# Prompt attention: the coefficients of the probabilities for two heads at a time, the first pair ahead

## Chip, cores and metric

The kernel runs on one core of a Trainium2 chip. The core has five engines that work side by side and wait for one another by semaphores: TensorE (PE: products of matrices, transposes; its loads of weights are shown as PEld), VectorE (DVE), ScalarE (ACT), GpSimd (POOL) and SyncE (SP, which issues DMAs). The metric is the device time of one execution in microseconds, as the median of several runs.

## What is computed

One step of a hybrid layer for a prompt of 1024 tokens and a decode batch of 8 sequences with 4 tokens each: a recurrent mixer, an attention with three branches, and a convolutional feed-forward. The change touches only the attention of the prompt, 8 query heads of width 64 in 2 groups that share keys and values:

```
def masked_softmax(s, mask):
    s = jnp.where(mask, s.astype(jnp.float32), -jnp.inf)
    m = jnp.max(s, axis=-1, keepdims=True)
    e = jnp.where(mask, jnp.exp(s - m), 0.0)
    d = jnp.sum(e, axis=-1, keepdims=True)
    return e / jnp.where(d > 0, d, 1.0)
...
    g = jax.nn.sigmoid(gate_raw.astype(jnp.float32)).reshape(B, T, 3, NSA_KV_HEADS, NSA_GROUP)[..., None]
    o = g[:, :, 0] * o_cmp + g[:, :, 1] * o_slc + g[:, :, 2] * o_win
```

The three branches attend to compressed keys, to selected blocks of keys (with 1024 tokens and 16 blocks of 64, all of them are selected) and to a window of 512 keys. Each branch's probabilities are divided by their sum d and weighted by a gate g; gate over sum is the coefficient that this document speaks of, one number for each query and head.

## The kernel before

`prompt_attention` works in units. For each of the 2 groups there is one unit for the compressed branch (C), and then for each tile of 128 queries, 0 to 7, one for the selected branch (S0, S1, ...) and one for the window (W0, W1, ...): 17 units in a group, 32 dense ones (S and W) in all. A dense unit has 4 heads (R) and a width u.w of 128 for each block of keys: 128 to 1024 for S, at most 640 for W.

A unit goes through these steps:
- Scores on PE (`scores`, L802 to L807), in fills of the two score tiles in PSUM, `ps`: one fill of four heads up to a width of 256, two fills of two heads up to 512, four fills of one head above. So S0 to W1 have one fill, S2 to W3 two, S4 to W7 four.
- Maximum on DVE (`maximum`, L717), negated into `nm`.
- Exponential on ACT (`probabilities`, L630), from the score tile into `Pr[u.dense % 3]` in SBUF, with the sum of each head put into `den` by the same operation.
- Coefficients on DVE (`coefficients`, L730 and L731): for four heads at once, the reciprocal of `den` in place, a wait on that (`cd`), and the product with the gates into `cf`. The wait in front is for all four heads' exponentials.
- Scaling on GpSimd (`scale`, L587): one operation for each head, in place in `Pr`, in the order of the units.
- For each block of 128 keys ("back"): four transposes on PE, one for each head, into a tile `pt` of PSUM (`turn`, L826; with the first block, the transpose of head h waits for the scaling of head h), a copy of the high part on ACT (`high_of`, L644, or L640 for compressed probabilities), the remainder on DVE (`rest_of`, L739), and two products with the values on PE (`values`, L846 and L847), two backs later. W units of an even tile have one back more, for the compressed probabilities of two tiles.
- After the last back of a W unit: the two halves of the sum are copied out of PSUM by ACT (L651) and DVE (L744) and added by DVE (L751) (`both_halves`).

The order of all this is written out by hand. Stage i (one pass of the outermost loop) interleaves the backs of unit i with the "fronts" (fills: scores, maximum, exponential) of unit i+2, by `merged(i)`; PE, ACT and DVE all go through the same list. Behind the first entry of stage i, which is a front if there is one, DVE makes the coefficients of unit i+1. ACT is one fill behind: it does an exponential behind the next back's copy, or in front of the next front.

For example, the list of stage S5, where the fronts are those of S6, is: f0 b0 b1 f1 b2 f2 b3 b4 f3 b5.

Of the kernel before, what the change touches and what calls it, by code (L numbers as in the profile page):

```python
# [9 lines left out]
ALU = mybir.AluOpType  # L10
# [14 lines left out]
R = NH // NG  # L25
# [427 lines left out]
def prompt_attention(nc, io, keep, scratch, consts_sb):  # L453
# [6 lines left out]
    CMP, SLC, WND = 0, 1, 2  # L460
    AHEAD = 2
# [4 lines left out]
    units = []  # L466
    n_fills = n_heads = n_groups = n_dense = 0
    for g in range(NG):
        for kind, qt in [(CMP, 0)] + [(kind, qt) for qt in range(NQ) for kind in (SLC, WND)]:
            u = Unit()  # L470
# [39 lines left out]
    with ExitStack() as ctx:  # L510
# [7 lines left out]
        mask, cmask, eye, gates = keep["mask"], keep["cmask"], keep["eye"], keep["gates"]  # L518
# [5 lines left out]
        den = sb("den", [P, NU, R])  # L524
        cf = sb("cf", [P, NU, R])
        nmc, denc, cfc = (sb(n, [P, NG, R, NQ]) for n in ("nmc", "denc", "cfc"))
        half = sb("half", [64, 512])
# [9 lines left out]
        s_ready, max_ready, e_ready, c_ready, p_ready = (sem(n) for n in ("s_ready", "max_ready", "e_ready", "c_ready", "p_ready"))  # L537
# [44 lines left out]
        @block.gpsimd  # L582
        def _(pool):
            def scale(u):
                pool.wait_ge(c_ready, u.dense + 1)
                for h in range(R):
                    nc.gpsimd.tensor_scalar(Pr[u.dense % 3][:, h, 0:u.w], Pr[u.dense % 3][:, h, 0:u.w], cf[:, u.n, h:h + 1], None,  # L587
                                            ALU.mult).then_inc(p_ready, 1)

            def scale_compressed(u):  # L590
                pool.wait_ge(cc_ready, u.g + 1)
                p3 = Pc[u.g][:].rearrange("p r t n -> p (r t) n")
                nc.gpsimd.tensor_tensor(p3, p3, cfc[:, u.g].rearrange("p r t -> p (r t)").unsqueeze(2).to_broadcast([P, R * NQ, CB]),
                                        ALU.mult).then_inc(cp_ready, 1)

            for u in units:
                if u.kind == CMP:
                    scale_compressed(u)
                else:
                    scale(u)  # L600
# [75 lines left out]
        @block.vector  # L676
        def _(dve):
            for e in range(4):
                dve.wait_ge(kH_ready, e + 1)
                at = (slice(None), e // 2, slice(512 * (e % 2), 512 * (e % 2) + 512))  # L680
                nc.vector.scalar_tensor_tensor(KT[1][:, 1][at], pt[e % 3][:].rearrange("p b c -> p (b c)"), SCALE, KT[1][:, 0][at].bitcast(F32),
                                               ALU.mult, ALU.subtract).then_inc(kL_ready, 1)

            def second_low(i):
                if i == 1:
                    for a in range(2):
                        dve.wait_ge(vH_ready, a + 1)
                        nc.vector.tensor_tensor(V2[1][:, a, :, DK:P], vv[:, a, :, DK:2 * DK], V2[1][:, a, :, 0:DK].bitcast(F32), ALU.subtract
                                                ).then_inc(vL_ready, 1)
                elif i in (2, 3):  # L690
                    for h in range(2 * i - 4, 2 * i - 2):
                        dve.wait_ge(qH_ready, h + 1)
                        nc.vector.tensor_tensor(Q[1][64:128, h, :], qs[h % 2][64:128, :], Q[1][64:128, h, :].bitcast(F32), ALU.subtract
                                                ).then_inc(qL_ready, 1)

            cs, cd = Steps(dve, cs_step), Steps(dve, cd_step)

            def maximum(u, b):
                s = ps[(u.fill0 + b) % 2]
                dve.wait_ge(s_ready, u.fill0 + b + 1)  # L700
                if u.kind == CMP:
                    s3 = s[:].rearrange("p (x n) -> p x n", n=CB)
                    m = nmc[:, u.g, 2 * b:2 * b + 2].rearrange("p r t -> p (r t)")
                    cs(nc.vector.tensor_reduce(m, s3, AX.X, ALU.max))
                    cs(nc.vector.tensor_scalar(m, m, -BIG / 1e10, None, ALU.max))
                    nc.vector.tensor_tensor(Pc[u.g][:, 2 * b:2 * b + 2].rearrange("p r t n -> p (r t) n"), s3,
                                            m.unsqueeze(2).to_broadcast([P, 2 * NQ, CB]), ALU.subtract).then_inc(cs_ready, 1)
                    return
                if u.per == 4:
                    src = s[:].rearrange("p (b x) -> p b x", b=2)[:, :, 0:2 * u.w].rearrange("p b (i w) -> p b i w", i=2)  # L710
                    dst = nm[:, u.n, :].rearrange("p (b i) -> p b i", b=2)
                elif u.per == 2:
                    src = s[:].rearrange("p (b x) -> p b x", b=2)[:, :, 0:u.w]
                    dst = nm[:, u.n, 2 * b:2 * b + 2]
                else:
                    src, dst = s[:, 0:u.w], nm[:, u.n, b:b + 1]
                nc.vector.tensor_reduce(dst, src, AX.X, ALU.max, negate=True).then_inc(max_ready, 1)  # L717

            def coefficients(u):
                if u.kind == CMP:  # L720
                    dve.wait_ge(ce_ready, u.fills * (u.g + 1))
                    d = denc[:, u.g].rearrange("p r t -> p (r t)")
                    cd(nc.vector.tensor_reduce(d, Pc[u.g][:].rearrange("p r t n -> p (r t) n"), AX.X, ALU.add))
                    cd(nc.vector.tensor_scalar(d, d, 1e-30, None, ALU.max))
                    cd(nc.vector.reciprocal(d, d))
                    nc.vector.tensor_tensor(cfc[:, u.g], denc[:, u.g], gates[:, :, R * u.g:R * u.g + R].rearrange("p t r -> p r t"),
                                            ALU.mult).then_inc(cc_ready, 1)
                    return
                dve.wait_ge(e_ready, u.head0 + R)
                cd(nc.vector.reciprocal(den[:, u.n, :], den[:, u.n, :]))  # L730
                nc.vector.tensor_tensor(cf[:, u.n, :], den[:, u.n, :], gates[:, u.qt, 8 * u.kind + R * u.g:8 * u.kind + R * u.g + R],  # L731
                                        ALU.mult).then_inc(c_ready, 1)

            def rest_of(u, k):
                G = u.group0 + k
                dve.wait_ge(h_ready, G + 1)
                src = pt[G % 3][:].rearrange("p b c -> p (b c)")
                hi, lo = (PcH[:], PcL[:]) if u.pair and k == u.groups - 1 else (PTH[:, G % 3, :], PTL[:, G % 3, :])
                nc.vector.tensor_tensor(lo, src, hi.bitcast(F32), ALU.subtract).then_inc(l_ready, 1)  # L739

            def both_halves(u):
                a = u.g * NQ + u.qt
                dve.wait_ge(pv_ready, pv_before[u.n])
                nc.vector.tensor_copy(lower[:], acc[0:64, :]).then_inc(lower_ready, 1)  # L744
                dve.wait_ge(half_ready, a + 1)
                dve.wait_ge(lower_ready, a + 1)
                if a >= 2:
                    dve.wait_ge(oT_out[a % 2], 16 * (a // 2))
                for odd in range(2):
                    at = lambda x: x.rearrange("p (k o c) -> p k o c", k=2, o=2)[:, :, odd]  # L750
                    nc.vector.tensor_tensor(oT[a % 2][64 * odd:64 * odd + 64], at(lower[:]), at(half[:]), ALU.add).then_inc(oT_ready, 1)  # L751

            for i in range(-AHEAD, NU + 1):
                order = merged(i)
                turned = 0
                for n in range(max(1, len(order))):
                    if order:
                        what, k = order[n]
                        if what == "back":
                            rest_of(units[i], k)  # L760
                            turned += 1
                            if turned == 2 and units[i - 1].kind == WND:
                                both_halves(units[i - 1])
                        else:
                            maximum(units[i + AHEAD], k)
                    if n == 0:
                        if 0 <= i + 1 < NU:
                            coefficients(units[i + 1])
                if turned < 2 and 1 <= i <= NU and units[i - 1].kind == WND:
                    both_halves(units[i - 1])  # L770
                second_low(i)
# [2157 lines left out]
```

## Time and profile before

| | |
|---|---|
| median of 3 runs | 2477.19 us (2475.43 to 2477.25) |
| profiled execution | 2471.7 us, its span 2469.9 us |
| PE busy in the span | 2281.8 us (92%) |
| DVE busy | 1305.3 us (53%) |
| ACT busy | 946.9 us (38%) |
| GpSimd busy | 513.2 us (21%) |
| prompt attention, dense units | 1212 us to 1518 us of the span |

The profile is of one execution. Times in its rows are counted from the start of the span. A row of the timeline gives the start, the time taken, the engine, the line of the kernel, the operation with its output and input, and in square brackets the idle time of the engine before it with the instruction that ended it; a row with no bracket had next to none. Names are those of the program without buffer numbers: `a_Pr` are the probabilities, `a_PTH` and `a_PTL` the high part and the remainder of a transposed block, `a_nm` the maxima, `a_den` the sums, `a_cf` the coefficients.

### The profile page before, as it was taken

The page shows a single profiled execution, that of the slowest core. Times are in us where ns is not written, and L with a number is a line of the kernel's source. Part 1 is how long each engine was busy: PE and PEld are TensorE (multiplying, and loading weights), DVE is VectorE, ACT ScalarE, POOL GpSimd, SP SyncE. Part 2 cuts the span into 40 slices and gives each one's busy share as a digit, 9 for nine tenths or more (in the row PEclk, how much of TensorE's full clock was granted, in tenths as well). Part 3 has the DMA queues.
Part 4 walks back from the last instruction along what each step waited for, and adds up shares of the span by engine and source line. Part 5 has one row for each costly group of instructions (what it writes and reads, how often), then busy time and mean ns, then how long its engine had stood idle before and what let it go on. Part 6 is the DMA issues. An engine that isn't in the chain of part 4 may idle for free. (4 is left out here: it accounts for less than half of the span.)

```text
span 2469.9 us, 40234 instructions
## 1 busy us (share of the span) xinstructions
PE 2281.8 (92%) x15950; PEld 2044.5 (83%) x15950; DVE 1305.3 (53%) x2960; ACT 946.9 (38%) x1911; POOL 513.2 (21%) x877
## 2 busy tenths in 40 slices
PE   6999989999999999669788885989999999999999
PEld 6999987777877777558667674869999999989998
DVE  5123028867767767643576775453333343355555
ACT  4124124545545545412365664112222222144444
POOL 0000005333433333200277673100000000011110
PEclk9999999999999999879699997999999999999999
DMA  4125626745546453297110002321111111122223
GB/s 133 52 64 174 241 97 222 229 157 177 174 154 207 154 177 94 56 300 216 41 41 7 10 7 94 109 73 48 51 42 51 43 45 49 51 77 82 79 70 116
DMA packets 213285, 263.10 MB, mean 107 GB/s; under 512 B 32386, under 2 KB 180098, under 8 KB 203746
## 3 DMA queue, kind: packets, MB, share of 16 engines
q1 hardware_dynamic: 194376, 157.61, 21.2%
q0 software_dynamic: 18752, 103.37, 12.1%
q8 instruction: 103, 1.69, 0.3%
q14 instruction: 54, 0.44, 0.1%
HBM read 202.76 MB, written 65.05 MB: 108 GB/s over the span
## 5 line engine op out<-in xcount | busy, mean ns | idle before, releaser
L1453 PE MATMUL f<-hH,wH 128*128 128x352 f32 x1056 | 341.4, 323 | 5.2 <-DVE wL L1339 5.2
L1453 PE MATMUL f<-hL,wH 128*128 128x352 f32 x1056 | 339.1, 321 | 0.0
L1453 PE MATMUL f<-hH,wL 128*128 128x352 f32 x1056 | 338.8, 321 | 0.0
L2406 ACT CAST a_XTH<-cpt 64x256 fp32r<-64x256 f32 (+1 forms) x576 | 201.1, 349 | 148.5 <-PE cpt L2613 137.9
L2523 DVE TENSOR_TENSOR a_XTL<-cpt,a_XTH 64x256 fp32r<-64x256 f32 (+1 forms) x576 | 230.3, 400 | 32.4 <-ACT a_XTH L2406 24.1
L1468 PE MATMUL f<-wdH,aH 128*128 128x256 f32 (+1 forms) x792 | 225.1, 284 | 5.3 <-DVE aL L1391 4.6
L1468 PE MATMUL f<-wdH,aL 128*128 128x256 f32 (+1 forms) x792 | 224.3, 283 | 0.0
L1468 PE MATMUL f<-wdL,aH 128*128 128x256 f32 (+1 forms) x792 | 224.3, 283 | 0.0
L587 POOL TENSOR_SCALAR a_Pr<-a_Pr,a_cf 128x640 f32<-128x640 f32 (+7 forms) x128 | 204.2, 1613 | 72.5 <-DVE a_cf L731 72.4
L2628 PE MATMUL cph<-a_XTH,a_w1H 128*128 128x512 f32 x512 | 217.4, 425 | 0.0
L2628 PE MATMUL cph<-a_XTH,a_w1L 128*128 128x512 f32 x512 | 205.3, 401 | 0.0
L2628 PE MATMUL cph<-a_XTL,a_w1H 128*128 128x512 f32 x512 | 204.4, 399 | 0.0
L1453 PEld LDWEIGHTS f<-hH,wH 128*128 128x128 f32 x1056 | 198.8, 188 | 5.3 <-DVE wL L1339 5.3
L1453 PEld LDWEIGHTS f<-hL,wH 128*128 128x128 f32 x1056 | 198.9, 188 | 0.0
L1453 PEld LDWEIGHTS f<-hH,wL 128*128 128x128 f32 x1056 | 198.5, 188 | 0.0
L1391 DVE TENSOR_TENSOR aL<-a_aT,aH 128x1408 fp32r<-128x1408 f32 (+1 forms) x72 | 108.2, 1503 | 122.7 <-ACT aH L1280 122.7
L1339 DVE TENSOR_TENSOR wL<-raw,wH 128x1024 fp32r<-128x1024 f32 x44 | 53.8, 1225 | 225.2 <-ACT wH L1242 222.8
L2231 POOL DMA_INDIRECT a_X<-in_cache_nsa_kv,idx x64 | 62.9, 983 | 425.7 <-issue 351.3
L1468 PEld LDWEIGHTS f<-wdH,aH 128*128 128x128 f32 (+1 forms) x792 | 144.0, 182 | 6.8 <-DVE aL L1391 5.2
L1280 ACT CAST aH<-a_aT 128x1408 fp32r<-128x1408 f32 (+1 forms) x72 | 91.4, 1270 | 147.5 <-PE f L1468 147.4
L1468 PEld LDWEIGHTS f<-wdL,aH 128*128 128x128 f32 (+1 forms) x792 | 144.0, 182 | 0.7
L1468 PEld LDWEIGHTS f<-wdH,aL 128*128 128x128 f32 (+1 forms) x792 | 143.9, 182 | 0.7
(459 smaller groups left out, 5377.3 us busy)
## 6 DMA issues: line engine op xcount, KB each, us to landing
v_s<-a_X SPq DMA_DIRECT2D x32, 512.0 KB, 6.4
raw<-in_w_in POOLq DMA_DIRECT2D x12, 1024.0 KB, 5.9
a_V<-v_s SPq DMA_DIRECT2D x6, 2048.0 KB, 15.0
raw<-in_w_gate SPq DMA_DIRECT2D x22, 512.0 KB, 3.8
raw<-in_w_val SPq DMA_DIRECT2D x22, 512.0 KB, 3.8
wraw<-in_w_down SPq DMA_DIRECT2D x44, 256.0 KB, 3.8
z_tok<-stage SPq DMA_DIRECT2D x48, 128.0 KB, 3.5
a_akq<-hq SPq DMA_DIRECT2D x32, 192.0 KB, 5.5
```

What stands on the lines that cost most here:

```text
L587: nc.gpsimd.tensor_scalar(Pr[u.dense % 3][:, h, 0:u.w], Pr[u.dense % 3][:, h, 0:u.w], cf[:, u.n, h:h + 1], None, ALU.mult).then_inc(p_read ...
L1280: nc.scalar.copy(aH[:, h, :, 0:r], aT[:, NFH * h:NFH * h + NFH, t * P:t * P + r]).then_inc(aH_ready, 1)
L1339: nc.vector.tensor_tensor(wL[:, a], raw[:, a], wH[:, a].bitcast(F32), ALU.subtract).then_inc(wL_ready, 1)
L1391: nc.vector.tensor_tensor(aL[:, h, :, 0:r], aT[:, NFH * h:NFH * h + NFH, t * P:t * P + r], aH[:, h, :, 0:r].bitcast(F32), ALU.subtract).th ...
L1453: last = nc.tensor.matmul(bank[3 * a + n][:, 0:w], wp[:, a, k, :], hp[:, k, c0:c0 + w], start=(k + part == 0), stop=(k == KD - 1 and part ...
L1468: last = nc.tensor.matmul(bank[t % 3][0:r, 0:QW], ap[:, h, j, 0:r], wp[:, f, :], start=(f + part == 0), stop=(f == NF - 1 and part == 2))
L2231: nc.gpsimd.indirect_dma_start(X[j % 3][:, half].rearrange("p t n -> p (t n)"), None, cache, bass.IndirectOffsetOnAxis(ap=idx[:, 2 * u + h ...
L2406: nc.scalar.copy(turned(XTH, u, s, k, g, a), split(bank(at, k)[:], u, k, g, a)).then_inc(h_ready, 1)
L2523: last = nc.vector.tensor_tensor(turned(XTL, u, s, k, g, a), split(bank(at, k)[:], u, k, g, a), hi.bitcast(F32), ALU.subtract)
L2628: last = nc.tensor.matmul(out[:, :, 0:n], w[:, k, q, s, m * P:(m + 1) * P], x[:, s % 2, k, :, q:q + n], **flags)
```

## The change

The coefficients of a dense unit are made for heads 0 and 1, and for heads 2 and 3, each pair with its own wait for its two exponentials and its own increment of `c_ready`. GpSimd waits for the first before head 0 and for the second before head 2. For units of more than one fill, the first pair moves from the stage after the unit's scores into the stage of its scores: it stands behind the entry that follows the unit's third front for four fills (`n + 1`), and behind the second entry after its second front, or at the end of the stage if that comes first, for two fills (`n + 2`). The second pair stays where the coefficients were. In units of one fill both pairs stand there.

```diff
@@ scale, on GpSimd
-                pool.wait_ge(c_ready, u.dense + 1)
                 for h in range(R):
+                    pool.wait_ge(c_ready, 2 * u.dense + 1 + h // 2)
                     nc.gpsimd.tensor_scalar(Pr[u.dense % 3][:, h, 0:u.w], Pr[u.dense % 3][:, h, 0:u.w], cf[:, u.n, h:h + 1], None,
                                             ALU.mult).then_inc(p_ready, 1)
@@ coefficients, on DVE
-                dve.wait_ge(e_ready, u.head0 + R)
-                cd(nc.vector.reciprocal(den[:, u.n, :], den[:, u.n, :]))
-                nc.vector.tensor_tensor(cf[:, u.n, :], den[:, u.n, :], gates[:, u.qt, 8 * u.kind + R * u.g:8 * u.kind + R * u.g + R],
-                                        ALU.mult).then_inc(c_ready, 1)
+                for half in range(2):
+                    if (u.n, half) not in weighted:
+                        pair_coefficients(u, half)
+
+            weighted = set()
+
+            def pair_coefficients(u, half):
+                hs = slice(2 * half, 2 * half + 2)
+                at = 8 * u.kind + R * u.g + 2 * half
+                weighted.add((u.n, half))
+                dve.wait_ge(e_ready, u.head0 + 2 * half + 2)
+                cd(nc.vector.reciprocal(den[:, u.n, hs], den[:, u.n, hs]))
+                nc.vector.tensor_tensor(cf[:, u.n, hs], den[:, u.n, hs], gates[:, u.qt, at:at + 2], ALU.mult).then_inc(c_ready, 1)
@@ the list of a stage, on DVE
-                turned = 0
+                turned, early = 0, None
...
-                            maximum(units[i + AHEAD], k)
+                            u = units[i + AHEAD]
+                            maximum(u, k)
+                            if u.kind != CMP and u.fills > 1 and k == u.fills // 2:
+                                early = (n + 1 if u.fills == 4 else n + 2, u)
+                        if early is not None and n >= early[0]:
+                            pair_coefficients(early[1], 0)
+                            early = None
                     if n == 0:
                         if 0 <= i + 1 < NU:
                             coefficients(units[i + 1])
+                if early is not None:
+                    pair_coefficients(early[1], 0)
```

## Rows read from the trace of the kernel before

**Rows 1.** Start:end, length, busy of PE, PEld, DVE, ACT, POOL, PE's clock, DMA

```profile
1212.00:1518.00 306.00, 252.88 (x1438) 206.77 (x1437) 225.99 (x355) 183.16 (x412) 211.39 (x130) 0.93 0.06 18
```

**Rows 2.** Waits, same stretch: total us, times, longest

```profile
POOL a_Pr L587 <- DVE a_cf L731: 72.4, 24, 8.0
...
DVE a_PTL L739 <- ACT a_PTH L644: 52.5, 65, 5.0
...
PE pt L826 <- POOL a_Pr L587: 34.4, 36, 3.3
```

**Rows 3.** GpSimd's groups by shape: busy us, mean ns, idle before

```profile
L587 POOL TENSOR_SCALAR a_Pr<-a_Pr,a_cf 128x896 f32<-128x896 f32 x8 | 20.1, 2527 | 10.1 <-DVE a_cf L731 10.1
```

**Rows 4.** Groups of DVE's instructions, same stretch and columns

```profile
L717 DVE TENSOR_REDUCE a_nm<-s 128x1 f32<-128x640 f32 (+7 forms) x87 | 83.2, 956 | 5.6 <-PE s L807 4.5
...
L731 DVE TENSOR_TENSOR a_cf<-a_den,gates 128x4 f32<-128x4 f32 x32 | 9.0, 281 | 1.1
...
L730 DVE RECIPROCAL a_den<-a_den 128x4 f32<-128x4 f32 x32 | 5.4, 169 | 0.1
```

**Rows 5.** Timeline around S6: start us, us, instruction, idle before

```profile
1304.77 0.69 DVE L739 TENSOR_TENSOR a_PTL<-pt,a_PTH 128x512 fp32r<-128x512 f32 x1
...
1309.30 0.17 DVE L730 RECIPROCAL a_den<-a_den 128x4 f32<-128x4 f32 x1
...
1309.50 0.16 DVE L731 TENSOR_TENSOR a_cf<-a_den,gates 128x4 f32<-128x4 f32 x1
...
1309.76 17.49 POOL L587 TENSOR_SCALAR a_Pr<-a_Pr,a_cf 128x896 f32<-128x896 f32 x8 [5.07 <-DVE a_cf L731]
...
1317.35 0.33 PE L826 MATMUL pt<-ident,a_Pr 128*128 128x128 f32 x1 [0.67 <-POOL a_Pr L587]
...
1319.85 0.33 PE L826 MATMUL pt<-ident,a_Pr 128*128 128x128 f32 x1 [2.17 <-POOL a_Pr L587]
...
1320.83 0.69 DVE L739 TENSOR_TENSOR a_PTL<-pt,a_PTH 128x512 fp32r<-128x512 f32 x1 [2.54 <-ACT a_PTH L644]
```

**Rows 6.** Timeline of DVE, GpSimd and PE around S7 of the second group

```profile
1483.02 0.68 DVE L739 TENSOR_TENSOR a_PTL<-pt,a_PTH 128x512 fp32r<-128x512 f32 x1
...
1488.42 11.32 POOL L587 TENSOR_SCALAR a_Pr<-a_Pr,a_cf 128x1024 f32<-128x1024 f32 x4 [7.90 <-DVE a_cf L731]
...
1499.79 0.47 PE L826 MATMUL pt<-ident,a_Pr 128*128 128x128 f32 x1 [2.49 <-POOL a_Pr L587]
...
1500.92 0.69 DVE L739 TENSOR_TENSOR a_PTL<-pt,a_PTH 128x512 fp32r<-128x512 f32 x1 [5.03 <-ACT a_PTH L644]
```

**Rows 7.** Timeline of DVE: first remainders of S4, S5; one amid W3's stage

```profile
1277.58 0.69 DVE L739 TENSOR_TENSOR a_PTL<-pt,a_PTH 128x512 fp32r<-128x512 f32 x1 [1.36 <-ACT a_PTH L644]
...
1297.71 0.69 DVE L739 TENSOR_TENSOR a_PTL<-pt,a_PTH 128x512 fp32r<-128x512 f32 x1 [0.59 <-ACT a_PTH L644]
...
1272.52 0.69 DVE L739 TENSOR_TENSOR a_PTL<-pt,a_PTH 128x512 fp32r<-128x512 f32 x1 [0.26 <-ACT a_PTH L644]
```

**Rows 8.** Timeline of DVE: first remainders of S2, first and second group

```profile
1245.51 0.69 DVE L739 TENSOR_TENSOR a_PTL<-pt,a_PTH 128x512 fp32r<-128x512 f32 x1 [2.31 <-ACT a_PTH L644]
...
1399.04 0.69 DVE L739 TENSOR_TENSOR a_PTL<-pt,a_PTH 128x512 fp32r<-128x512 f32 x1 [1.69 <-ACT a_PTH L644]
```

**Rows 9.** Timeline of DVE: first remainders of S3 and S7, first group

```profile
1260.56 0.69 DVE L739 TENSOR_TENSOR a_PTL<-pt,a_PTH 128x512 fp32r<-128x512 f32 x1
...
1348.19 0.68 DVE L739 TENSOR_TENSOR a_PTL<-pt,a_PTH 128x512 fp32r<-128x512 f32 x1
```

**Rows 10.** Timeline of GpSimd and DVE: scalings, and output sums beside them

```profile
1299.08 5.61 POOL L587 TENSOR_SCALAR a_Pr<-a_Pr,a_cf 128x640 f32<-128x640 f32 x3
...
1301.00 1.00 DVE L751 TENSOR_TENSOR a_oT<-a_lower,a_half 64x256 f32<-64x256 f32 x1
...
1348.37 7.47 POOL L587 TENSOR_SCALAR a_Pr<-a_Pr,a_cf 128x640 f32<-128x640 f32 x4 [1.82 <-DVE a_cf L731]
...
1350.96 0.87 DVE L751 TENSOR_TENSOR a_oT<-a_lower,a_half 64x256 f32<-64x256 f32 x2
```

## Prediction

> **Names.** S6 is the unit of the selected branch for query tile 6, W6 the window unit that follows it; the order is S0, W0, S1, W1 and so on, once for each group of heads. While unit i is turned and used, the scores of unit i+2 are made; at the start of that stretch VectorE makes the coefficients of unit i+1, and GpSimd scales its four heads. An entry of the hand-written order is a "back" (transpose, copy, remainder, product of one block) or a "front" (scores, maximum, exponential of one fill).
>
> **What bounds the kernel now.** First I read the busy time of the stretch that the change touches [rows 1]: 306 us, in which PE is busy 253, DVE 226, GpSimd 211, ACT 183. No engine is full, so waits decide. The waits [rows 2] show a chain: PE's transposes wait 34.4 us for GpSimd's scaling, ACT waits for PE, and DVE waits 52.5 us for ACT's copies. So a late scaling idles all three. But a wait of PE is worth only what the next engine also idles: DVE works in a fixed order, and where its next remainder comes straight behind its coefficients, PE's wait was hidden. So I read the timeline at each unit's first transpose, PE's idle time and then DVE's idle time before its first remainder.
>
> S6 is the clear case [rows 5]: its coefficients start at 1309.30, GpSimd scales head after head at 2.53 us [rows 3], PE stands at head 2 for 0.67 us and at head 3 for 2.17 us, until 1319.85, and DVE stands 2.54 us until 1320.83.
>
> **What the change adds.** The reciprocal and product over four heads become two pairs of the same instructions over two heads. The reciprocal took 0.17 us on average [rows 4], the product 0.16 us in S6 [rows 5] (its mean of 0.28 comes from a few that were held up, below). Nearest row for two elements is the same pair for four, which bounds it from above, and nothing from below but 0; since so few elements can hardly be what takes the time, I take the upper end: from 1309.30 to 1309.66 [rows 5], with the gap between the two, 0.37 us. 32 units times 0.37 = 11.8 us more on DVE. The new wait in front of the first pair has behind it all that DVE does: remainders and maxima. ACT does the exponentials of the first two heads before the copy that DVE's preceding remainder has already waited for, so by the order this wait is always over; price 0, or the rival below. GpSimd's second wait sits between heads 1 and 2 and holds nothing that wasn't held before.
>
> **What it moves.** Units of one fill (S0, W0, S1, W1) get no lead. In units of two fills (S2, W2, S3, W3) the first pair stands at the end of the stretch, one maximum ahead. In units of four fills (S4 to W7) it stands two to four entries ahead. Take S6: the pair comes behind the fourth remainder, 1304.77 + 0.69 = 1305.46, and is done at 1305.85; two heads until 1310.9, the second pair has been there since 1309.7, two more heads until 1316.0. PE came to head 2 at 1316.68 [rows 5], so nothing is left of the wait. What is late next is DVE itself: its S7 maximum and the second pair end near 1318.1. Gain = DVE's idle time, 2.54 us.
>
> **The sum of gains, by DVE's idle time.**
> - S6: 2.54, in both groups (the second repeats the first; one row stands for both): 5.1.
> - S4 1.36 and S5 0.59 of DVE's idle time [rows 7], with the pair some 2.6 us earlier (a maximum, a remainder, a maximum: 2 x 0.96 [rows 4] + 0.69 [rows 7]): 2 x 1.95 = 3.9.
> - S7 of the second group [rows 6]: the last but one unit; nothing is left to overlap. PE waits for heads 2 and 3 until 1499.79, DVE 5.03 us until 1500.92. The first pair would come behind the remainder at 1483.02, so at 1484.1, and four heads of 2.83 us end at 1495.4 instead of 1499.7: 4.3.
> - S7 of the first group: the remainder starts at 1348.19 with no idle time before it [rows 9], behind the long work on the next group's compressed scores: 0.
> - S3: the same, the remainder at 1260.56 has no idle time before it [rows 9]: 0, though PE waits here.
> - S2: idle 2.31 and 1.69 [rows 8]. In front of it DVE has 3 more pairs by then (W1, S2, W2), 1.1 us, which these gaps swallow; left are 1.2 and 0.6. The lead, one maximum of 0.96 [rows 4], moves all four heads by about that much, in the first group by more, since the copies of the second group's queries lie between. 1.8.
> Gross: 5.1 + 3.9 + 4.3 + 0 + 1.8 = 15.1 us.
>
> **The costs on the path.** Between S2 and S4 DVE and ACT pass work back and forth with no slack (maximum, exponential, copy, remainder), so the pairs of S3 and W3 cost their full 0.37: 4 x 0.37 = 1.5. In the wide units DVE has about 0.26 us or more idle before each remainder (the last of [rows 7]); that hides a pair in two backs. That cover would be gone if PE got faster there, which nothing here does. S0, W0, S1: DVE waits for copies right behind, 0.
>
> **The shared port.** A product of DVE with both inputs in SBUF can be held by GpSimd. In [rows 10] the second half of an output sum takes 1.00 us instead of 0.42: GpSimd began a head at about 1300.95 (the second of three in 5.61), and DVE got through some 0.6 us later. But the two sums at 1350.96 took 0.87 together, so 0.43 each, in the middle of a head: only the beginning of a head holds DVE. The first pairs now fall while GpSimd may be busy. Bounds for each of the 24: 0 and 0.6; a third of a head's time, GpSimd busy half of the time, gives about 0.1, so 2.4 us on DVE, of which a fifth on the path: 0.5.
> The Trainium skill, "SBUF — State Buffer", section "Who interferes with whom", says that the one that comes second is blocked for the whole instruction. The sums at 1350.96 speak against that for this scaling. By that rule an early pair would be held for the rest of a head; the price of that is a rival below.
>
> **The clock.** The stretch has 0.93 of the full clock [rows 1], so about 306 x 0.07 x 2 = 43 us of it at the lower level, 1.2 GHz. Most of that lies at its start and end, some 3 to 7 us behind long waits of PE (S6, S7). An estimate: if the gone waits take these with them, between 0 and 3 us; I take 1.
>
> **Sum.** 15.1 - 1.5 - 0.5 = 13.1, and with about 1 us from the clock, 14 us. The profiled execution took 2471.7 us (span 2469.9 and 1.8 around it), 5.5 under the median of 2477.19; nothing in the gain depends on that difference. Predicted: 2471.7 - 14 = 2457.7 for such an execution, 2477.2 - 14 = 2463.2 for the median.
>
> **The rivals.**
> - *DVE becomes the bound.* All 32 pairs are on the path, because with GpSimd's lateness gone DVE has no idle time to swallow them: 15.1 - 11.8 - 0.5, about 3 us gain, 2474. For it: DVE is at 226 of 306 [rows 1]. Against: 0.26 us idle per back even in the wide units [rows 7], and 52.5 in all before remainders [rows 2]. Chance 0.10; by size it counts as "same".
> - *All of PE's waits come back,* S3 and S7 of the first group too, and the clock with them: PE waits 34.4 in all [rows 2], of which about 12 stand at one-fill units and can't come back (added up from the timeline); 22.5, less 1.5 for the pairs and with 1 from the clock, is 22 us, 2455. Against: DVE's rows at S3 and S7. Chance 0.10.
> - *It doesn't lead.* GpSimd is still at the unit before when the first pair comes, so the heads move by nothing, and the pairs cost 1.5 to 2: 2479, no change. For S6 the unit before is done at 1299.08 + 5.61 = 1304.7 [rows 10], 1.2 us before the pair. Chance 0.04.
> - *The port holds DVE for whole heads (slower).* Place: the 24 early products. Each would be held by half a head on average, 7.47 / 4 / 2 = 0.93 us [rows 10], where GpSimd is busy; if that is always and on the path, 24 x 0.93 = 22, against 15.1 - 1.5: 9 us slower, 2486. It decides from 0.6 us a product. Against it: the sums at 1350.96 [rows 10]. Chance 0.04. (This is what the rule of the Trainium skill, "SBUF — State Buffer", would give.)
> - *The new wait isn't over (slower).* If DVE stood for an exponential and its sum, about 1 us, in 24 units, 24 us: 2487. Against: the order on ACT. Chance 0.03.
> - The forecast: 0.69.
>
> **How the numbers follow.** The likeliest case gives 2463.2. Its own range is 10 to 19 us gain: the low end if the port takes all of 24 x 0.6 x a third on the path, the high end with S2's full idle times and clock back. The range of 8 in 10 takes in the all-waits case and the DVE-bound one: 2455 to 2474; outside are the cases without a lead and the slower ones, and the tails. A measurement of this kernel tells about 0.2%, 5 us, from no change. Faster by more: 0.69 + 0.10 + a little of the DVE-bound case, 0.81. Within: 0.08 of that case and 0.04 without a lead, 0.12. Slower by more: 0.04 + 0.03 = 0.07.
>
> **What would show it.** Right: the reciprocal 64 times; GpSimd's wait for coefficients well under 72 us [rows 2]; PE's wait for scaling down by about 20 us from 34.4, with what is left at S0 to W2; DVE's 2.54 before S6's remainder and 5.03 before S7's gone; the stretch at 306 down to about 292. Wrong: DVE's early products at 1 us or more; DVE idle on ACT's exponentials in front of the new reciprocals; or PE's waits for scaling replaced one for one by waits for DVE's remainders.

## The result, and the profile after

The changed kernel took 2454.60 us (median of 4, 2450.86 to 2457.48) against 2477.22 us before (median of 4): ratio 0.9909, interval 0.9892 to 0.9926. That is 22.6 us faster where 14 were forecast, and 0.4 us below the low end of the range, 2455.0. In two later measurements the same kernel gave 15.0 and 14.8 us (below); all executions together, 42 of before and 14 of after, have means of 2474.4 and 2457.7: 16.7 us, with about 2 us of uncertainty (two standard errors). So the sign was right and the size was forecast somewhat too small. The first measurement lies above the later ones.

Waits of the changed kernel in the attention, 1215 to 1501 us of its span, in the columns of [rows 2], and then the busy time in those of [rows 1]:

```profile
POOL a_Pr L587 <- DVE a_cf L741: 46.5, 20, 4.9
DVE a_PTL L748 <- ACT a_PTH L644: 25.4, 43, 1.7
PE pt L843 <- POOL a_Pr L587: 12.4, 16, 3.3
```

```profile
1215.00:1501.00 286.00, 246.16 (x1439) 203.59 (x1437) 232.56 (x420) 183.84 (x412) 212.20 (x130) 0.95 0.06 19
```

PE's wait for the scaling fell from 34.4 to 12.4 us and DVE's wait for copies from 52.5 to 25.4, while DVE is busy 6.6 us more. S6 in the changed kernel, DVE and GpSimd, to be read against [rows 5]:

```profile
1303.52 0.16 DVE L740 RECIPROCAL a_den<-a_den 128x2 f32<-128x2 f32 x1
1303.71 0.16 DVE L741 TENSOR_TENSOR a_cf<-a_den,gates 128x2 f32<-128x2 f32 x1
1303.96 17.64 POOL L587 TENSOR_SCALAR a_Pr<-a_Pr,a_cf 128x896 f32<-128x896 f32 x8 [3.45 <-DVE a_cf L741]
1307.44 0.15 DVE L740 RECIPROCAL a_den<-a_den 128x2 f32<-128x2 f32 x1
...
1315.96 0.69 DVE L741 TENSOR_TENSOR a_cf<-a_den,gates 128x2 f32<-128x2 f32 x1
1316.58 0.68 DVE L748 TENSOR_TENSOR a_PTL<-pt,a_PTH 128x512 fp32r<-128x512 f32 x1
1317.61 0.69 DVE L748 TENSOR_TENSOR a_PTL<-pt,a_PTH 128x512 fp32r<-128x512 f32 x1 [0.35 <-ACT a_PTH L644]
```

The first pair is there 3.9 us ahead of the second, GpSimd starts at once and goes through eight heads (S6 and W6) with no break, and S6's first remainder has no idle time before it: the 2.54 us are gone. The product right in front of it takes 0.69 us instead of 0.16; that is the shared port, below. The first remainder of S7 of the second group, against [rows 6]:

```profile
1483.90 0.69 DVE L748 TENSOR_TENSOR a_PTL<-pt,a_PTH 128x512 fp32r<-128x512 f32 x1 [0.83 <-ACT a_PTH L644]
```

5.03 us of idle time have become 0.83.

**How the stage is measured.** From here on "the stage" is the time from the first remainder of S0 in the first group to the last one of W7 in the second: 294.9 us before, 274.3 after, 20.6 less. Starts of remainders are compared one by one; the step of a unit is what the two kernels' distance grows by from the end of the unit before it to its own last remainder (positive: saved). What lies behind the stage took 955 to 957 us in every profile. What lies ahead of it, which the change hardly touches (one pair of S0), took 1219.3 us in the profile before and 1221.0 to 1227.5 in the others, so whole times of single executions say less than the stage. Each stage is that of one execution, also the 294.9 us of before; where a run below has no ratio, it was executed once.

| unit | forecast, both groups | change, first group | change, second |
|---|---|---|---|
| W0, S1, W1 (second: and S0) | 0 | -0.7 | -0.9 |
| S2 | 1.8 | 2.5 | 1.2 |
| W2, S3, W3 | -1.5 | 0.3 | 0.4 |
| S4, W4 | 2.7 | 2.1 | 2.1 |
| S5 | 1.2 | 0.8 | 0.8 |
| S6 | 5.1 | 3.4 | 3.3 |
| S7, W7 | 4.3 | 0.7 | 4.7 |
| port, clock | +0.5 | in the rows above | |

Sum forecast 14 us, measured 20.6 us.

### The profile page after: what moved, and what is told of

Its sections match the earlier page's. It is cut to its first block and busy times, and to the rows that moved or that the text cites. A ratio compares the mean times of both kernels' runs of the same rounds, so it can differ in the third digit from the quotient of the medians.

```text
span 2452.9 us, 40298 instructions
## 1 busy us (share of the span) xinstructions
PE 2281.7 (93%) x15950; PEld 2046.8 (83%) x15950; DVE 1312.0 (53%) x3024; ACT 947.8 (39%) x1911; POOL 514.0 (21%) x877
```

## The experiments

**No lead at all, and the lead in one class of units.** First only the split of the coefficients, with both pairs at the old place:

```diff
-                            if u.kind != CMP and u.fills > 1 and k == u.fills // 2:
+                            if False:
```

> All coefficients are made for two heads at a time, but both pairs of a unit stand where the four heads' coefficients stood before; no pair is early. I measure the stage as the time from S0's first remainder on DVE to W7's last: 294.9 us before, 274.3 after the change, so 20.6 gained. Theory A (the gain comes from the lead alone, and a pair costs next to nothing): 294 to 297 us, DVE idle 2.5 us again before S6's first remainder, 5.0 before S7's in the second group, device time within 3 us of the kernel before. Rival B (the split itself gives a good part, since GpSimd no longer waits for all four heads): 283 to 290. Rival C (a pair costs its full 0.33 us wherever it stands): 304, 10 us slower than before.

Measured: ratio 1.0008 (0.9998 to 1.0017), 2476.73 against 2474.07 us. The stage is 296.8 us, 1.9 us longer than before. PE waits 31.3 us for the scaling, and S7 of the second group is late again:

```profile
1505.26 0.69 DVE L748 TENSOR_TENSOR a_PTL<-pt,a_PTH 128x512 fp32r<-128x512 f32 x1 [4.98 <-ACT a_PTH L644]
```

So the split gives nothing (rival B falls), and 32 more pairs cost 2 us, not 10 (rival C falls); the lead is the whole gain. The 2 us are a sum with PE's clock in it: S3 loses 1.6 and 0.7 us here, where the granted clock was 0.50 for 3.4 us, which it wasn't in the profile before, and S7 of the first group gains 1.8. The run with one early pair (below) has the same pairs, loses nothing at S3 of the first group, and without S7's step comes to 2.0 us again.

Then the lead for four fills alone, and for two fills alone:

```diff
-                            if u.kind != CMP and u.fills > 1 and k == u.fills // 2:
+                            if u.kind != CMP and u.fills == 4 and k == u.fills // 2:
```

> The first pair is early only in units of four fills (S4 to W7); in S2 to W3 both pairs stand at the old place. Theory A (the terms of the sum are separate): the stage keeps the steps of S4 2.0, S5 0.8, S6 3.4 in each group, S7 1.4 less 0.7 in the first and 4.7 in the second, 17.8 in all less what the split costs in the narrow units; 276.5 to 279 us. Rival D (the two-fill units' pairs cost 1.5 us on the path, as predicted, and their gain at S2 is 1.8): 274.5, no difference to the whole change.

Measured: stage 279.1 us, 15.8 less than before; S4 2.0, S5 0.8, S6 3.4 and 3.3, S7 of the second group 4.8, each within 0.1 of the change. Theory A holds to 0.1 us.

> The first pair is early only in units of two fills (S2, W2, S3, W3). Theory A: only the steps at S2 (2.5 and 1.2) and S3 (0.4 each) stay, with the losses of the one-fill units against them: stage 291 to 293 us. Rival D (the pairs of S3 and W3 are on the path at 0.37 each): 294.5. If 20.6 minus this gain and that of the run with the wide units alone is more than 1 us either way, the terms are not separate.

Measured (`u.fills == 2` in that line): stage 293.1 us, 1.8 less than before; S2 2.0 and 1.2, S3 0.5 and 0.5, nothing at S4 and S5. Counted from the run without a lead, 17.7 and 3.7 make 21.4 of the whole 22.5: the terms add up, to 1.1 us. By the rule that I had set down they don't, since 20.6 less 1.8 less 15.8 is 3.0; but both runs pay the 1.9 us of the split, which that rule counts twice. In the 1.1 stand 3.4 us at S7 of the first group and -2.0 at S3, where the clock fell at other times in these runs. Rival D's "no difference" to the whole change falls, and so does its 294.5: the pairs of S3 and W3 don't cost 0.37 each.

**One unit alone, and a short lead.** In this run only S7 of the second group has its first pair early (`u.kind == SLC and u.g == 1 and u.qt == 7` in the same line):

> The first pair is early in one unit only, S7 of the second group; all others have both pairs at the old place. Theory A (each unit's lateness is its own term): the stage is that of the run with no early pair, 296.8 us, less S7's step of 4.7 us: 292 us; all other units' steps stay within 0.1 of that run, but for those where the clock differs. Rival F (S7's step is so large only because S6 and W6 were early and GpSimd came free): less than 3.5 us from S7.

Measured: stage 292.2 us; S7's step against the run without a lead is 4.7 us, and its first remainder has 0.83 us of idle time before it, as in the change. One early pair of two tiny instructions is worth 4.7 us, by itself (rival F falls). That all other units stay within 0.1 doesn't hold: S3 is 1.6 and 0.8 us shorter than in the run without a lead, and S7 of the first group 1.8 longer; the clock fell at other places in the two (at 1263.5 and 1417.1 there, not here).

```diff
-                                early = (n + 1 if u.fills == 4 else n + 2, u)
+                                early = (len(order), u)
```

> The first pairs of the four-fill units too stand at the end of the stage, so that their lead is one maximum (0.8 to 1.2 us) instead of two to four entries (2.6 to 5 us). Theory A (a unit gains the smaller of its lead and its lateness): S5, late by 0.7 us, keeps its 0.8; S4, late by 1.3, keeps 1.2 to 2.0; S6, late by 2.8, keeps about 1.2 to 1.6 of 3.4; S7 of the second group, late by 4.7, about 1.2 of 4.7. Stage 274.3 + 2 x 2 + 3.5 + 0 to 1.5 = 281 to 284 us. Rival G (what counts is that GpSimd starts on two heads before the other two have their coefficients, not by how much): 274 to 277 us.

Measured: stage 290.6 us, steps against the run without a lead S4 0.86, S5 0.7, S6 0.7 and 0.8, S7 1.5. The lead is here one maximum of 640 columns, 0.81 us, for all of them, and S4 to S6 are cut to about that, as the smaller of lead and lateness. S7's first remainder comes 0.9 us earlier; the rest of its 1.5 comes at the second one, where W7's pairs and the clock differ too. S7's idle time is what is left over:

```profile
1498.76 0.69 DVE L748 TENSOR_TENSOR a_PTL<-pt,a_PTH 128x512 fp32r<-128x512 f32 x1 [3.82 <-ACT a_PTH L644]
```

I had expected somewhat more at S4 and S6, and a stage of 281 to 284; of the 7 to 10 us that are missing, 4.6 are at S7 and W7 of the first group, measured against the change, where PE's clock fell for 13.65 us (below); most of the others come from my having put the lead at up to 1.2 us instead of 0.81. Rival G falls: what counts is by how much GpSimd starts earlier.

**The cost of a pair where it stands.** Behind each early pair one more of the same kind, into a spare tile:

```diff
+                if half == 0 and u.fills > 1:
+                    cd(nc.vector.reciprocal(spare[:, 0], gates[:, u.qt, at:at + 2]))
+                    cd(nc.vector.tensor_tensor(spare[:, 1], spare[:, 0], gates[:, u.qt, at:at + 2], ALU.mult))
```

> The whole change, and behind each of the 24 early pairs one more reciprocal and one more product of the same two-element size, each waited for, into a tile that nobody reads: the cost of a pair is doubled where it stands. The instructions take about 0.2 us each from start to start, 0.4 us a pair, 9.6 us in all. Theory A (DVE's slack takes them in the wide units, only those in S2 to W3 count): stage 274.3 us plus 0 to 3. Rival C (DVE has become the bound with the scaling no longer late): 282 to 285 us.

Measured: stage 282.8 us, 8.5 more than the change. By units: 5.7 us at S7 and W7 of the first group, where PE's clock was at its lower level for 17 us; S2, W2 and S3 0.8, 0.4 and 0.7 in the first group; W2 and S3 0.4 and 0.7 in the second (and 0.7 at W1, given back at S2); S4 0.35, which W4 gives back (0.4); nothing above 0.25 at S5 to W7. So without the clock 2.8 of some 9 us, nearly all in units of two fills. The 0.8 at S2 may not be the pairs': the changed kernel, unaltered, lost the same there in its second profile (below). Theory A holds for the wide units, by the steps; the total alone would have spoken for rival C.

**The window units.** Pairs and leads only for S2 to S7; all window units, S0 and S1 have their four coefficients in one go:

```diff
+    def paired(u):
+        return u.kind == SLC and u.fills > 1
...
-                            if u.kind != CMP and u.fills > 1 and k == u.fills // 2:
+                            if paired(u) and k == u.fills // 2:
```

> Pairs, the first of them early, only in the selected units of more than one fill (S2 to S7); all window units and S0, S1 have their four coefficients in one go, as before the change: 12 instead of 32 extra pairs. Theory A (only the selected units had PE waiting for the scaling; the window units' early pairs buy nothing): the stage is as short as with the whole change or shorter by what 20 pairs cost, 271 to 274.5 us. Rival E (an early window pair frees GpSimd for the selected unit behind it, so it takes part in the lead): GpSimd gets to S4, S6 and S7 later, 277 us or more.

Measured: 2454.45 us, ratio 0.9921 (0.9903 to 0.9939), stage 274.4 us. S4 and S6 keep their steps, S5 gains 0.5 more in each group and S7 of the second 0.6, W7 behind it loses 1.0. The window units' early pairs buy nothing but at the very end, so rival E falls. The 0.5 at S5 is the shared port: the two output sums in its stage take 1.32 us with the change and 0.84 here, since GpSimd's heads start at other times. With the last window unit paired too:

> The run with pairs only in the selected units, with one more pair in the last window unit, which lost 1.0 us there; all other window units and S0, S1 in one go. Theory A: steps as in that run, without the loss at W7: stage 273.5 us with the same clock, at most 1 us better than the change, which no measurement of this kernel can tell: ratio to the kernel before 0.989 to 0.993, and within its interval of the change's.

Measured: 2456.27 us, ratio 0.9926 (0.9899 to 0.9952), stage 273.8 us, the shortest of all. No measurement of the whole kernel tells it from the change.

**The waits that are left.** Of the 12.4 us, 9.7 stand at one-fill units. Here DVE scales their heads itself:

```diff
+                if u.fills == 1:
...
+                    for h in range(R):
+                        x = Pr[u.dense % 3][:, h, 0:u.w]
+                        nc.vector.tensor_scalar(x, x, cf[:, u.n, h:h + 1], None, ALU.mult).then_inc(n_ready, 1)
```

> The whole change, and in the one-fill units (S0, W0, S1, W1 of both groups) DVE itself scales the four heads behind their coefficients, made in one go there; GpSimd scales the wider units only. PE's waits for scaling that are left after the change stand mostly here (about 10 of 12 us). Theory A: a head of 128 or 256 columns takes DVE 0.2 to 0.4 us against 0.62 and 0.94 on GpSimd, so PE waits 2 to 5 us less and the stage is 270 to 272.5 us, the device time 2 to 5 us below that of the change. Rival H (DVE is what bounds the narrow units, and 8 x 4 more operations there cost 8 us against the 5): 275 to 278 us.

Measured: 2460.03 us, ratio 0.9938 (0.9915 to 0.9961), stage 279.2 us; 4.8 of the 4.9 us above the change are at S7 and W7 of the first group (clock at the lower level for 13.65 us), the one-fill units come out even. A head takes DVE 0.32 us on average, and PE now waits for DVE there:

```profile
PE pt L861 <- DVE a_Pr L742: 5.7, 3, 2.9
```

PE's wait for the scaling is 8.5 us here instead of 12.4, and yet theory A's 2 to 5 us don't come, nor rival H's loss. That the start of a one-fill unit waits for its whole chain, not for the speed of the scaling, is my reading; no run shows it by itself.

**The port.** The product of a pair by two operations that have one input tensor in SBUF each and take the gate as a scalar:

```diff
-                nc.vector.tensor_tensor(cf[:, u.n, hs], den[:, u.n, hs], gates[:, u.qt, at:at + 2], ALU.mult).then_inc(c_ready, 1)
+                for j in range(2):
+                    h = 2 * half + j
+                    last = nc.vector.tensor_scalar(cf[:, u.n, h:h + 1], den[:, u.n, h:h + 1], gates[:, u.qt, at + j:at + j + 1], None, ALU.mult)
+                last.then_inc(c_ready, 1)
```

> The whole change, but the product of a pair is made by two operations of one head each, that have one input tensor in SBUF and take the gate as a scalar, in place of one operation with two input tensors. In the profile after the change 12 of 64 products took 0.3 to 0.8 us instead of 0.16, and each of these began shortly behind the start of one of GpSimd's heads. Theory P (GpSimd holds a second input of DVE in the first third of a head, and nothing else): all products take 0.1 to 0.2 us, W4's first remainder no longer loses 0.55 us (it gets it back at the next one, so the total stays), stage 272 to 275 us where the clock is the same. Rival Q (any operation of DVE is held, or the products wait for their reciprocals): the same operations are long again.

Measured: the product in the change, and then here (duration in ns, min/median/max):

```profile
L741 DVE TENSOR_TENSOR a_cf<-a_den,gates x64: 160/161/3007, 1215.7 to 1484.7; 128x2 f32<-128x2 f32 x64
```

```profile
L743 DVE TENSOR_SCALAR a_cf<-a_den,gates x128: 200/210/215, 1214.4 to 1491.6; 128x1 f32<-128x1 f32 x128
```

Not one of 128 is held. S4's first remainder, the coefficients before it in the change, and here:

```profile
1277.05 0.77 DVE L741 TENSOR_TENSOR a_cf<-a_den,gates 128x2 f32<-128x2 f32 x1
1277.74 1.43 DVE L748 TENSOR_TENSOR a_PTL<-pt,a_PTH 128x512 fp32r<-128x512 f32 x2
```

```profile
1276.87 0.34 DVE L743 TENSOR_SCALAR a_cf<-a_den,gates 128x1 f32<-128x1 f32 x2
1277.12 0.68 DVE L751 TENSOR_TENSOR a_PTL<-pt,a_PTH 128x512 fp32r<-128x512 f32 x1
1278.30 0.69 DVE L751 TENSOR_TENSOR a_PTL<-pt,a_PTH 128x512 fp32r<-128x512 f32 x1 [0.50 <-ACT a_PTH L644]
```

Without the hold S4's first remainder is 1.3 us earlier than before instead of 0.84, and the second one gains 0.2 instead of 0.64: what the port takes, the next idle time gives back. The unit's sum stays. Theory P holds for the products, rival Q falls. The stage was 282.3 us, 8.0 more than the change: 4.7 us at S7 and W7 of the first group (clock at the lower level for 13.65 us), 1.0 at S3 of the second group, where the clock fell again, and 2.3 in small steps elsewhere. So without the clock it is some 277, not the 272 to 275 expected; the two operations take 0.34 us together, a product that isn't held 0.16.

**How large is it really?** The changed kernel twice more, unaltered:

> The changed kernel once more, unaltered, beside the kernel before on the same chip. Theory A: ratio 0.990 to 0.993; all steps of the units as in the first profile within 0.1 us, except at S7 of the first group, where the clock falls and where five runs so far differed by up to 6 us. Rival K (a good part of the first measurement was luck with the clock): ratio 0.994 to 0.996, with PE at the lower level for 10 us or more between 1345 and 1380 us in this profile.

Measured: 2457.86 us against 2472.88, ratio 0.9943 (0.9925 to 0.9962), stage 276.3 us. All units' steps are those of the first profile within 0.1 us, but for S2 of the first group (0.8 less; the clock fell there at 1242.9 us, in the first profile at 1245.0) and S7 of the first group (1.4 less).

> The changed kernel a third time, unaltered, in five rounds beside the kernel before: the first measurement gave 22.6 us, the second 15.0. The steps that repeat to 0.1 us in every profile (S4 2.0, S5 0.8, S6 3.4 in each group, S7 of the second 4.8, S2 and S3 some 3.5 together, one-fill units -1.7) add up to 19; what varies is PE's clock at the change of groups (S7 of the first group: 0 to 5 us). Theory A: gain 17 to 20 us, ratio 0.992 to 0.993. Rival K (the second measurement was the true one, and the clock at the change of groups is worse with the change in most executions): 13 to 16 us, ratio 0.9935 to 0.995.

Measured: 2459.18 us against 2473.99, ratio 0.9936 (0.9921 to 0.9950), so 14.8 us; stage of the profiled execution 278.4 us, 4.1 above the first profile: 4.5 us more at S7 of the first group, 0.3 less at W1, all else within 0.1. Rival K's times are met in both measurements. PE's clock near the wait there, in the first profile of the change (two stretches) and in the last (one), columns as in [rows 1]:

```profile
1350.80:1354.20 3.40, 3.40 (x16) 3.10 (x16) 2.38 (x3) 0.59 (x1) 0.00 (x0) 0.50 0.02 5
1354.20:1364.40 10.20, 7.50 (x50) 6.16 (x50) 8.18 (x13) 5.47 (x15) 1.72 (x1) 1.00 0.00 0
```

```profile
1349.80:1363.40 13.60, 12.90 (x53) 11.95 (x54) 5.15 (x8) 1.63 (x3) 1.77 (x1) 0.50 0.04 11
```

In both, PE stood for 3.45 us for DVE's copy of the sum. In the first the wait ended at 1345.79 and the clock fell 5 us later; in the last it fell at 1349.8, while PE stood:

```profile
1350.50 0.76 PE L863 MATMUL acc<-a_PTH,V2a 128*128 128x512 f32 x1 [3.45 <-DVE a_lower L753]
```

## Why the prediction was right in sign and small in size

**What bounds the kernel, and what is late next: right.** The lateness of GpSimd is where the time was: without a lead nothing changes, with one pair early one unit alone gives its 4.7 us. DVE's order decides what PE's wait is worth. DVE's idle time before the first remainder priced it well: with no product held at the port the first remainders moved by 1.3 at S4 (forecast 1.36) and 2.8 at S6 (2.54; before the change W6's product in front of it took 0.45 us, held for the 0.29 that make the difference), and by 0.7 at S5 (0.59) and 4.2 at S7 of the second group (4.3).

**The shared port: the step that failed.** The sum has it as a cost of 0.5 us, for the early products. In the change these are indeed held, but that costs nothing in the end: the first two remainders together move by 1.48 us at S4 and 2.94 at S6, with held products as without. What I left out is that an earlier GpSimd also moves the holds that the kernel before had. The two output sums in S4's stage, before and then in the change:

```profile
1280.33 1.43 DVE L751 TENSOR_TENSOR a_oT<-a_lower,a_half 64x256 f32<-64x256 f32 x2
```

```profile
1279.85 0.87 DVE L760 TENSOR_TENSOR a_oT<-a_lower,a_half 64x256 f32<-64x256 f32 x2
```

S4's third remainder gains 0.57 us by that, in each group. It does so in each of the 9 profiles in which S4 has its full lead, and in none of the 5 others, in which the sums take 1.40 us as before. The same gives 0.3 in each group at S3, 0.1 in each at S5, and in the second 0.2 at S6 and 0.1 at S7. All 32 sums took 17.4 us before and 15.1 after. With the 0.3 us of W6's product in each group the port gave back some 2.8 us where the sum had a cost of 0.5. These 3.3 us are half of the 6.6 that the forecast lacks against the stage of the first profile.

**The cost of pairs on the path: mis-sized too.** W2, S3 and W3 were to lose 1.5 us; they gain 0.7. Single remainders do lose, 0.17 us at S3's first and 0.24 at W3's (where a product is held, and the next remainder gets it back), 1.2 us in all. Against this stand 1.9: S3's second remainder had 0.26 us of idle time before it and gains 0.35, a row behind the one that I had read, and the sums give their 0.3. The reading beneath the term was wrong: the last of [rows 7] stands in W3's stage and shows 0.26 us of slack just where I said there was none, while in the wide units half of the 96 remainders had less than 0.2 us idle before them. The run with extra pairs shows nevertheless that pairs cost in the units of two fills and hardly in the wide ones. A pair is 0.27 us from its start to the next instruction's (the row of the next overlaps its end) rather than 0.37, and in the run without a lead 32 of them cost 1.9 us.

**S2 and the one-fill units: right together.** S2 gained 3.6 instead of 1.8, and the one-fill units, which I had at 0, lost 1.6. I had taken the pairs in front of S2 off its gain; they cost in front of it. The sum is 2.0 against 1.8.

**The clock: about right.** In the profile before, PE was at 1.2 GHz for 3.4 us behind S6's first transposes and for 6.8 us around those of S7 of the second group; in the change it wasn't. At S6 of the first group DVE's copy of the sum waited for PE's products there, which took 0.63 us each and 0.40 in the change:

```profile
1322.77 0.63 PE L851 MATMUL acc<-a_PcL,VC 128*128 128x512 f32 x1
...
1323.44 0.68 DVE L744 COPY a_lower<-acc 64x512 f32<-64x512 f32 x1 [0.33 <-PE acc L851]
```

That wait is gone, and most of the 0.42 us that S6's third remainder gains is this; S2 of the first group gains 0.37 in the same way. At S7 of the second group four transposes in front of the second remainder took 1.05 us before and 0.60 in the change, and it gains 0.47. All this is some 1.2 us; I had taken 1.

**S7 of the first group: right at first, and then the clock.** The first three blocks moved by 0.0, as forecast; in the first profile S7 and W7 still gained 0.7, in the two others of the change they lost 0.7 and 3.7. PE's wait for the scaling, 0.95 us, and its wait for DVE's copy, 2.28, became one of 3.45 us. What follows differs from one execution to the next: 3.4 us at 1.2 GHz and short stretches later, or 13.65 us in one piece. Over 14 profiles of all kernels, the time from S7's first remainder to that of the next group's W1 is 43 to 46 us with first falls of 3.4 to 10.2 us and 49 to 51 us with the long ones of 13.65 us and more. A long one was seen in 5 of 10 profiles in which S7 of the first group had a lead, and in none of the 4 in which it had not. That the single longer wait makes the long fall likelier is a guess from these few; no run changed that wait alone. The three profiles of the change have stages of 274.3, 276.3 and 278.4 us, so 20.6, 18.6 and 16.5 less than the one of before, which agrees with 16.7 us over all executions and its uncertainty of 2. That the two later measurements, 15.0 and 14.8 us, lie next to the forecast of 14 is in part luck: the steps ahead of S7 are larger than forecast in all three profiles, and the clock at the change of groups took some of it back. Of the difference between 22.6 us and the two later 15, about 2.5 us lie in the first sample of before (mean 2477.0, later ones 2473.5 to 2474.6); how the rest divides between the clock and what lies ahead of the stage stays open.

**The rule for a hold.** By the Trainium skill, "SBUF — State Buffer", section "Who interferes with whom", a one-input operation outside the modes with two ports isn't held, which the 128 products of 0.20 to 0.215 us bear out; that a hold lasts for the whole of GpSimd's instruction isn't what the rows show: S4's product was let through 0.65 us into a head of 1.88 us.

**The range.** It ended at 22 us gain, with the chance of 0.10 for "all of PE's waits come back". PE's wait for the scaling did come down by 22.0 us, and the stage of the first profile by 20.6. But that rival's way wasn't the one: S3 and S7 of the first group gave only part of their waits, and the port gave much of the rest. "DVE becomes the bound", "it doesn't lead" and both slower rivals are excluded by the runs.

## What to carry to other kernels

Where one engine feeds another through a helper that is late at each unit's start, give the helper the first half of its inputs as soon as they exist; the gain of each unit is the smaller of lead and lateness, and it can be had for two tiny instructions in an engine that looks busy. Price it by the idle time that the last engine of the chain has in front of its first late instruction. Then look at what shares a port with the helper: when the helper's starts move, its holds move with them, those that you add and those that you had. A wait removed in front of another wait may join it: then the time lies there. When single executions differ by 5 us, compare the starts of the same instruction unit by unit; those repeated here to 0.1 us where PE's clock was the same.

## What the runs showed of the hardware

- A hold at the port grows with the width of GpSimd's head, not with DVE's operation: products of two elements that came at the start of a head ended 0.59 us behind its start at 384 columns (1.25 us long), 0.81 at 640 (1.89), 0.92 at 768 (2.21) and 1.13 at 1024 (2.85); with the 0.16 us of the product taken off, 0.43 to 0.97 us, about a third of the head. GpSimd's two-input product of 2048 columns (3.61 us) held one for 3.0 us, to its end. An output sum of 64x256, 0.42 us by itself, took up to 1.0 us when one of GpSimd's heads began just before it or during it.
- At two elements instead of four the reciprocal took 0.156 us instead of 0.169 and the product 0.16 in both: at this size the length doesn't matter.
- Near the same wait of 3.45 us PE's clock was at 1.2 GHz once for 3.4 us and once for 13.65 us, with the same program.
